# Two tiles' scaled one-hots on ScalarE, gate chunks between u blocks, two staging places, prompt v rows in three parts

## The reference

```python
q = (x @ w_q).reshape(n, PEER_HEADS, 2, PEER_HALF)
s1 = jnp.einsum('nhd,kd->nhk', q[:, :, 0], key1)
s2 = jnp.einsum('nhd,kd->nhk', q[:, :, 1], key2)
t1, i1 = lax.top_k(s1, 16); t2, i2 = lax.top_k(s2, 16)
cand = t1[..., :, None] + t2[..., None, :]
top, pos = lax.top_k(cand, 16)          # 16 experts (i1, i2) of each head
g = jax.nn.softmax(top, axis=-1)
a = jnp.einsum('thkd,td->thk', u_tab[ib], xb)
w = gelu(a) * gb
out = jnp.einsum('thk,thkd->td', w, v_tab[ib])
```

## Time and profile before

| | us |
|---|---|
| median of 3 runs | 4348.91 |
| the profiled execution | 4340.14 |
| its span | 4338.2 |
| PE busy | 3703.1 (85%) |
| DVE busy | 3035.8 (70%) |
| POOL busy | 1601.5 (37%) |
| ACT busy | 561.0 (13%) |
| DMA, mean of the span | 291 GB/s |

### The profile page before, as it was taken

The page is one execution under the profiler, slowest core; times in us unless marked ns, Lnnn a source line. Parts: engine busy times, 40 slices in busy tenths (PEclk is TensorE's granted clock), DMA queues, the critical chain, the costliest instruction groups (busy, mean ns, idle before and its releaser), DMA issues.

```text
span 4338.2 us, 38925 instructions
## 1 busy us (share of the span) xinstructions
PE 3703.1 (85%) x12854; PEld 2276.6 (52%) x12854; DVE 3035.8 (70%) x6633; ACT 561.0 (13%) x1373; POOL 1601.5 (37%) x1290
## 2 busy tenths in 40 slices
PE   8985858899999688989996767799999869998897
PEld 5534434478888533434443534347788753443343
DVE  0016887687975988766664797768896689766667
ACT  0011022111112300000001113111112130000000
POOL 0000753334412143755540175143341304555453
PEclk9787867999999899999997876899999899999998
DMA  6663964589988598999994496468998849999996
GB/s 229 201 228 105 364 219 160 203 291 385 352 300 301 201 347 287 390 398 394 395 350 151 160 339 220 141 252 281 364 384 287 299 181 337 333 396 395 396 392 241
DMA packets 470519, 1263.26 MB, mean 291 GB/s; under 512 B 39848, under 2 KB 143016, under 8 KB 464168
## 3 DMA queue, kind: packets, MB, share of 16 engines
q0 software_dynamic: 184320, 671.17, 41.2%
q1 hardware_dynamic: 260656, 505.71, 33.2%
q10 hardware_dynamic: 25344, 83.90, 4.8%
HBM read 1173.79 MB, written 86.84 MB: 291 GB/s over the span
## 4 chain that ended last, share of the span: by engine, by line
PE 42%; DVE 33%; DMA 18%; POOL 3%; issue 3%; ACT 1%; SPq 0%; DVEq 0%; ACTq 0%
DMA w_ring<-in_peer_v_dram 10%; PE P L769 9%; DVE ring L1020 7%; PE P L742 7%; PE P L720 6%; DMA ring<-in_peer_u_dram,eidx 4%; PE T L769 4%; DVE late L1038 3%; PE P L589 3%; POOL ring L509 3%; DVE h L1170 3%; PE P L532 3%; PE P L529 3%; DMA h<-acts_d 2%; DVE h L1166 2%
## 5 line engine op out<-in xcount | busy, mean ns | idle before, releaser
L509 POOL DMA_INDIRECT ring<-in_peer_u_dram,eidx x768 | 943.7, 1229 | 1766.3 <-DVE ring L1020 860.0
L769 PE MATMUL P<-w_ring,area 128*128 128x512 f32 x2048 | 955.8, 611 | 134.2 <-DMA w_ring<-in_peer_v_dram 74.4
L1020 DVE SCALAR_TENSOR_TENSOR ring<-ring,h 128x1024 f32<-128x1024 f32 x768 | 920.3, 1224 | 127.0 <-DMA ring<-in_peer_u_dram,eidx 121.3
L509 POOL DMA_INDIRECT ring<-in_peer_v_dram,eidx x512 | 655.8, 1281 | 919.4 <-DVE late L1038 448.8
L742 PE MATMUL P<-hT,w_ring 128*128 128x256 f32 x4096 | 900.5, 380 | 18.1 <-ACT late L899 18.1
L742 PEld LDWEIGHTS P<-hT,w_ring 128*128 128x128 f32 x4096 | 774.7, 191 | 123.3 <-ACT late L899 20.1
L769 PEld LDWEIGHTS P<-w_ring,area 128*128 128x128 f32 x2048 | 399.8, 196 | 651.2 <-issue 567.5
L769 PE MATMUL T<-w_ring,hT 128*128 128x512 f32 x1024 | 480.2, 592 | 0.0
L1038 DVE SCALAR_TENSOR_TENSOR h<-ring,dots,h 128x1024 f32<-128x1024 f32 x254 | 326.1, 1284 | 55.2 <-DMA ring<-in_peer_v_dram,eidx 43.7
L1038 DVE SCALAR_TENSOR_TENSOR late<-ring,dots,late 128x1024 f32<-128x1024 f32 x254 | 325.8, 1283 | 18.6 <-DVE late L1038 0.9
L769 PEld LDWEIGHTS T<-w_ring,hT 128*128 128x128 f32 x1024 | 194.6, 190 | 245.5 <-issue 245.5
(11 more groups left out here) (183 smaller groups left out, 3069.3 us busy)
## 6 DMA issues: line engine op xcount, KB each, us to landing
w_ring<-in_peer_uT_dram SPq DMA_DIRECT2D x256, 512.0 KB
w_ring<-in_peer_v_dram SPq DMA_DIRECT2D x256, 512.0 KB
area<-in_w_mod_dram SPq DMA_DIRECT2D x96, 512.0 KB, 4.6
gate_d<-area ACTq DMA_DIRECT2D x48, 1024.0 KB, 4.6
w_ring<-in_peer_wq_dram SPq DMA_DIRECT2D x64, 512.0 KB
acts_d<-late ACTq DMA_DIRECT2D x128, 256.0 KB
h<-acts_d SPq DMA_DIRECT2D x64, 512.0 KB
w_ring<-in_w_in_dram SPq DMA_DIRECT2D x48, 512.0 KB
```

The costliest lines, as they stand in the source:

```text
L509: pool.indirect_dma_start(out=ring[:, b, :], out_offset=None, in_=tables["uv".index(phase)], in_offset=bass.IndirectOffsetOnAxis(ap=eidx[: ...
L769: mm = pe.matmul(bank[ACC[2 * t + half]][:, :], w, uv_ring[:, held[b], half * 512:(half + 1) * 512], start=b == 0, stop=b == KEYS - 1)
L1020: dve.scalar_tensor_tensor(ring[:, b, :], ring[:, b, :], 1.0, h2[:, k, :], ALU.mult, ALU.mult, accum_out=dots[:, k, row:row + 1]).then_inc ...
```

## The change

- `u_order()` is written anew. Tile 3's 32 chunks come after u blocks 47 to 86 (before: 76 to 119), tile 4's after 88 to 119 (before: all after block 127), and six of tile 1's after 122 to 127. The three `slT` come after blocks 45, 87 and 121 (before: 64, 121 and behind tile 4's chunks).
- For tiles 3 and 4 ScalarE builds `oh_a` itself: four Abs of (number - index), a semaphore wait, four Relu of (weight - weight x distance), so eight instructions of 128 columns a chunk. It builds for chunk q + 2 behind its copy of chunk q. VectorE keeps only the tensor_tensor for these tiles. Tile 1's one-hots stay as they were.
- `gate_st` had both its halves in `area`. Now the even half is in `area` and the odd one in columns 0 to 255 of each of `hT`'s eight parts, so that an odd store takes 8 pieces of 1 KB a partition and an even one a piece of 8 KB.
- VectorE's order: one row dot a step instead of two while tile 3 is chosen; one dot and one one-hot a step while tile 4 is chosen; two dots a one-hot for tile 3's last ten; three dots a one-hot for tile 4's first 22. The prompt's v rows 64 to 95 are added between tile 1's one-hots, one each, and rows 96 to 127 in the first 32 v blocks, one a block instead of two.
- Three waits for softmaxes on ScalarE stand at other blocks.

```diff
+PV_LATE = 96
...
-        if b == 64:
+        if b == 45:
             order.append(("slT", 3))
-        if 76 <= b < 100 and b % 2 == 0:
-            order.append(("g", 3, (b - 76) // 2))
-        if 100 <= b < 120:
-            order.append(("g", 3, 12 + b - 100))
+        if b == 87:
+            order.append(("slT", 4))
         if b == 121:
-            order.append(("slT", 4))
-    order += [("g", 4, q) for q in range(CHUNKS)]
-    return order + [("slT", 1)] + [("g", 1, q) for q in range(CHUNKS)]
+            order.append(("slT", 1))
+        order += [("g", 3, q) for q in range(22) if 47 + 4 * q // 3 == b]
+        if 77 <= b < 87:
+            order.append(("g", 3, b - 55))
+        if 88 <= b < 120:
+            order.append(("g", 4, b - 88))
+        if b >= 122:
+            order.append(("g", 1, b - 122))
+    return order + [("g", 1, q) for q in range(KEYS - 122, CHUNKS)]
...
+        gate_st = [area[:, 2048:4096].rearrange("p (c n) -> p c n", c=DC), hT[:, :, 0:2 * P]]
...
+                def scaled_hots(k, q):
+                    n = V_DENSE.index(k) * CHUNKS + q
+                    for j in range(QUAD):
+                        t = q * QUAD + j
+                        act.activation(oh_a[:, n % 2, j, :], iota128, ACT.Abs, bias=slotT[:, 0, t:t + 1]).then_inc(oha_far, 1)
+                    act.wait_ge(oha_far, (l * len(U_DENSE) * CHUNKS + n + 1) * QUAD)
+                    for j in range(QUAD):
+                        t = q * QUAD + j
+                        ins = act.activation(oh_a[:, n % 2, j, :], oh_a[:, n % 2, j, :], ACT.Relu,
+                                             scale=slotT[:, 3, t:t + 1], bias=slotT[:, 2, t:t + 1])
+                    ins.then_inc(oha_ready, 1)
...
-                        if b == 24:
+                        if b == 20:
                             top_softmax(1)
-                        if b == 44:
+                        if b == 40:
                             top_softmax(3)
-                        if b == 100:
+                        if b == 70:
                             top_softmax(4)
...
+                        if k in U_DENSE and q + 2 < CHUNKS:
+                            scaled_hots(k, q + 2)
...
                 for i in range(2 * PH + 6):
-                    dot_rows(1, 2 * i, 2 * i + 2)
+                    dot_rows(1, i, i + 1)
                     choosing(3, i)
                 slots_out(3)
-                for i in range(2 * PH):
+                for i in range(2 * PH + 6):
+                    dot_rows(1, 22 + i, 23 + i)
+                    one_hots(3, i)
+                    choosing(4, i)
+                for i in range(10):
+                    one_hots(3, 22 + i)
                     dot_rows(1, 44 + 2 * i, 46 + 2 * i)
...
                 slots_out(4)
                 for i in range(CHUNKS):
-                    if i < 10:
-                        dot_rows(1, 108 + 2 * i, 110 + 2 * i)
                     one_hots(4, i)
+                    dot_rows(1, min(64 + 3 * i, SLOTS), min(67 + 3 * i, SLOTS))
                 slots_out(1)
                 for i in range(CHUNKS):
                     one_hots(1, i)
+                    add_rows(0, PV_EARLY + i, PV_EARLY + i + 1)
                 for b in range(KEYS):
                     weights_T(b)
                     if b < 32:
-                        add_rows(0, PV_EARLY + 2 * b, PV_EARLY + 2 * b + 2)
+                        add_rows(0, PV_LATE + b, PV_LATE + b + 1)
```

More of the change, by code:

```diff
@@ L328, in build @@
         oh_ready = sem("oh_ready")
+        oha_far = sem("oha_far")
+        oha_ready = sem("oha_ready")
         act_out = [sem(f"act_out{i}") for i in range(2)]
@@ L1165, in one_hots @@
                     ts = slice(q * QUAD, (q + 1) * QUAD)
-                    dve.tensor_tensor(oh_b[:, n % 2], slotT[:, 1, ts].unsqueeze(2).to_broadcast([P, QUAD, KEYS]),
-                                      iota128.unsqueeze(1).to_broadcast([P, QUAD, KEYS]), ALU.is_equal)
-                    for j in range(QUAD):
+                    ins = dve.tensor_tensor(oh_b[:, n % 2], slotT[:, 1, ts].unsqueeze(2).to_broadcast([P, QUAD, KEYS]),
+                                            iota128.unsqueeze(1).to_broadcast([P, QUAD, KEYS]), ALU.is_equal)
+                    for j in range(0 if k in U_DENSE else QUAD):
                         t = q * QUAD + j
```

40 lines of the change are left out of this document (22 added, 18 removed).

## The result

The changed kernel takes 4364.02 us (median of 14 runs, 4349.02 to 4374.13). The kernel before, on the same chip in the same session, takes 4344.83 (14 runs, 4339.28 to 4352.16). The ratio is 1.0039, with a 95% interval of 1.0028 to 1.0050: slower by about 17 us (19 by the two medians). The execution that the profiler recorded took 4369.6 us, with a span of 4367.6.

The account below looks back on a forecast made before the run. TensorE was taken to set the pace in the u stage and VectorE in the gates' end. To the first v block 26 us more, less 14 in the v stage, made 12 a layer, 24 in all: 4373 us, range 4325 to 4410.

Parts of the forecast that it names:

- TensorE's own work: Up to the last u block: 128 blocks, 70 chunks and three transposes, 505.5 us a layer without waits.
- Step 1: First transpose, now after block 45: TensorE waits 7 us for VectorE's dots, choice and weights of tile 3.
- Step 2: Choice for tile 4 between tile 3's one-hots: VectorE falls behind, TensorE waits 11 us, bounds 0 and 21.
- Steps 3 and 4: Tile 4's chunks: late rows from full DMA, 20 us; odd gate stores in small packets holding ScalarE's Gelu, 8 us.
- Step 5: TensorE's clock in the u stage: slow restarts after waits, four at 1.8 us, 7 us a layer.
- Step 6: ScalarE's eight new ops a chunk: 2.05 us, 3.0 of 4.34 with Gelu and copy, so hidden at no cost.
- ScalarE becomes the bound: Rival: ScalarE without slack after held stores, each costing TensorE 2 us more; 12 us a layer more, 4397; chance 0.18.
- The gates' end: Behind the last u block: 26 chunks, each with a one-hot pair and a row sum, 2.92 us each, 75.9 us.
- The v stage: Fewer row sums in the first 32 blocks put VectorE ahead before tile 2's choice: 14 us off, bounds 5 and 22.
- The traffic doesn't hold: Rival for the u stage: no waiting for rows, free engines for stores, fewer restarts; 32 us less a layer, 4309; chance 0.17.
- gains and costs cancel: Rival: row traffic and small-store waits half as large, 14 us less a layer, 4345; chance 0.15.
- The statement under the sum: Row sums cost TensorE little in the v stage, but 26 x 1.29 = 33 us among tile 1's one-hots.

Follow-up runs that it names:

- spread: Changed kernel with tile 1's row dots spread: two a step beside tile 4's searches and two instead of three beside its chunks; 4355.13 us, ratio 1.0034.
- both_spread: Changed kernel with late prompt rows added beside tile 2's choice again, odd gate blocks from 5 stored in 8 KB packets, row dots spread; 4276.63 us, ratio 0.9854.
- short_rows: Changed kernel with tile 1's expert rows 64 to 127 gathered with 1 KB a token instead of 4 KB; 4326.43 us, ratio 0.9961.
- half_hots: Changed kernel with ScalarE building only two of each chunk's four scaled one-hots of tiles 3 and 4; 4357.76 us, ratio 1.0038.
- all_half: both_spread with ScalarE building only two of each chunk's four scaled one-hots of tiles 3 and 4; 4274.83 us, ratio 0.9838.
- spread_half: spread with ScalarE building only two of each chunk's four scaled one-hots of tiles 3 and 4; 4342.94 us, ratio 1.0001.
- rows_only: Kernel before with only the row sums moved: 32 of 64 late prompt rows added among tile 1's one-hots; 4385.54 us, ratio 1.0101.
- adds_back: Changed kernel with prompt rows 64 to 95 added beside tile 2's choice again; 4339.71 us, ratio 0.9996.

## Why the prediction was right, point by point

The forecast was 4373 us, 24 more than before; the change is slower by 17 in the timed runs and by 29 in the profiled ones. The mechanisms that it named are there. That the sum comes so near is partly luck, since misses cancel: the waits of the u stage were put at 46 us and measure 38.3 and 40.8, the clock was put at 7 and took about 19 and 11.

- **TensorE's own work, 505.5 us.** Layer 0: 564.8 less 38.3 us of waits leaves 526.5, so 21 us are left for the clock (layer 1: 560.2 - 40.8 - 505.5 = 14).
- **Step 1, the transpose.** 7 predicted; 7.7 and 9.1 measured. Right.
- **Step 2, the choice for tile 4.** 11 predicted; three waits, 9.4 and 10.2 us. Right.
- **Steps 3 and 4, rows 20 and small stores 8.** Both mechanisms are there. DMA was at a share of 1.02 with 403 GB/s, and VectorE waited 30.3 us for rows in tile 4's part of layer 0. Behind an odd store, an activations' store issued at 1329.76 let its Gelu go at 1351.11, 21 us later (24 in spread). The prediction saw that the holds fall into the waits for rows and took 8 us for them, but it still counted 28 for both as a sum, and they don't add: each is hidden behind the other. Together they and their restarts are worth 29 us a layer (changed kernel to both_spread), singly 4 and 1. The waits of tile 4's part are 18.5 and 21.4 us, not 28, and its length 176 is 30 over TensorE's work once the clock is counted. Chunks with a u block came 5.7 us apart over the first 21 periods, 5.3 predicted. One bound was missed, that lies close under DMA's: GpSimd needs 5.2 us for three rows beside these dots (short_rows). In the changed kernel it mostly stands and waits for a free slot (23 of its 30 gathers from 1340 to 1400 us), so there DMA is the slower.
- **Step 5, the clock.** Four restarts of 1.8 us, 7, were too few, and in layer 0 too cheap. Layer 0's u stage has eight places where a chunk or block runs slow, at 1.6 to 3.0 us each, 19 in all; layer 1's has six, at 1.6 to 2.1, 11 in all. The rest of the 21 and 14 is no clock: it is some 0.17 us for each wait, by which the modelled end of a block (3.62 in the earlier trace rows) lies behind the next start (3.45). Not only the long waits are followed by such a place: one stands behind a wait of 2.40 us at 1388.39, with 1.80 us for the chunk. The 1.8 was read in the v stage.
- **Step 6, ScalarE.** 2.05 us a chunk predicted from one op of 128 columns, the Exp of a softmax; it is 2.9, over the upper bound of 2.5. An Abs takes 0.32 and a Relu 0.40. With Gelu and copy it is 3.6 to 3.8 us of 4.34, so the new work is still hidden (half_hots, all_half). The rival "ScalarE becomes the bound" is wrong in the kernel as changed. Its mechanism, put at 2 us more for TensorE at each held store, showed as 1.5 to 4.3 in spread_half against spread, where the rows no longer hide it.
- **The gates' end.** 75.9 predicted, 72.7 and 72.9 measured: a chunk takes 2.82, since the sum starts 1.19 us before the next instruction, not 1.29. The gap was put at 15, with 1 for small packets, and is 17.5. Most of the growth comes with the sums: rows_only, without a small packet, has 16.7, and adds_back, with them and without the sums, 14.7.
- **The v stage.** 14 off predicted, 18 and 11 measured; rows_only puts it at 15 and 19. (Layer 1's v stage before is 731.3 us, not the 732.8 that the prediction read: the stretch in the earlier trace rows runs on past its last product.)
- **The rivals.** "The traffic doesn't hold" is wrong, "gains and costs cancel" too. The statement under the sum, that the row sums cost 33 us here, is what decides: adds_back takes just them back and is level with the kernel before. All the rest of the change, 38 more chunks between u blocks and the scaled one-hots of two tiles on ScalarE, is worth nothing as it stands, and 1.5% once rows and stores are out of its way.

## What to carry to other kernels

When work is moved into a stretch where DMA, a store queue and an in-order engine are all near their limit, price each limit but don't add them: relieve two together before you call either harmless. Work that one engine can hide in one stage may cost its whole time in another, so look at who sets the pace where it lands. And where other queues keep the DMA engines full with larger packets, a store in many small ones delays what is queued behind it by their number, not by their bytes.
